# A plan of 26 rounds in place of 27 for the experts of a mixture, with a first batch of two rounds

## The chip, the cores and the metric

The kernel runs on one core of a Trainium2 chip. The metric is the device time of one execution in microseconds (us), the median of several runs. A profile was taken of one execution; its trace gives every instruction of the engines: PE (TensorE, matrix products), DVE (VectorE), ACT (ScalarE), POOL (GpSimd), and SP (SyncE), which here only issues DMAs.

## The reference

One layer of a backbone on 384 tokens (128 of context, 256 latent) of width 1024: a state space branch, a Fourier branch, and a mixture of 64 experts, of which a router gives six to each token. Only the mixture matters here:

```
scores = sigmoid(x @ w_router); idx = the six best of the four best groups
gates  = scores of idx, normed, * 2.5, else 0                 # (T, 64)
a = einsum("td,edf->tef", x, w1); b = einsum("td,edf->tef", x, w3)
act = silu(a) * b * gates[:, :, None]
routed = einsum("tef,efd->td", act, w2)                       # w1, w3: 1024x256, w2: 256x1024
x += gate2 * (routed + shared(x));  y = rms_norm(x)
```

All is float32. One expert's w1, w3 and w2 are 1 MiB each.

## The kernel before

Everything up to the router takes the first 490 us or so and is not touched. The last block of the kernel runs over the experts.

**Rounds and places.** Experts are sorted by how many tokens they got. A round is a tile of 128 rows (slots), which one to three experts share in blocks of 32 rows: `KINDS` has A with three experts of 2, 1, 1 blocks, B with two of 3 and 1, C with one of 4, D with two of 2 and 2. `PLAN` is a list of batches, each a string of rounds. Numbering the experts of the plan in order gives the places 0 to 63; `laid_out` gives the place with the most blocks to the expert with the most tokens. An expert with more tokens than its blocks hold would have the rest done by a dynamic loop (`Tail4`) behind the batches; on these inputs that loop runs no time. The plan of before has 27 rounds: three in the first batch, four in each of the six others.

**A batch** on PE: the gather (`L1700`: 48 matmuls, a column for each slot of the batch, takes the tokens of the slots out of H), then for each round p `hidden(p)` (`L1663`, w1 and w3 side by side, 1024 by 512), `turned(p)` (`L1670`, transposes), `slot_rows(p)` (`L1651`), `down(p)` (`L1684`, w2), and the scatter of two rounds at a time (`L1640`: six products of 512 columns to banks 0 and 1), whose results DVE adds to the sum (`add`, `L1828`). In a batch of four rounds the scatter of rounds 0 and 1 stands between `hidden(3)` and `down(2)`; that of rounds 2 and 3 comes in the next batch behind its `hidden(0)`. In the first batch of three, the scatter of rounds 0 and 1 stands behind `hidden(2)`.

The gather of a batch waits for the slots that DVE makes in `next_slots()`, and until the adds of the scatters issued before it are done (`pe.wait_ge(acc_ok, bt(12, -5))`).

**The weights.** Five slots of 3 MiB (`RING = 5`, the last is `sb_W`) hold the experts; place n lies in slot n % 5. The first four are loaded before the block. SP issues all other loads in program order, and stops at each whose slot is not free:

```
if place >= RING:
    sp.wait_ge(h_mm, round_of[place - RING] + 1)      # gate_up: w1 and w3
...
if place >= RING:
    sp.wait_ge(y1_mm, round_of[place - RING] + 1)     # downward: w2
```

For a batch of four rounds the order is gate_up 0, gate_up 1, downward 0, gate_up 2, downward 1, gate_up 3, downward 2, downward 3. Behind the last load SP waits for the last user of `sb_W` and issues there the stored activations (`x2_dram`, 1.5 MiB), the final gain (0.5 MiB) and, after that user's `down`, the gate `g2b` (1 MiB).

**The end.** In the last batch DVE does `add`, `before_residual(0)` (which waits for those three loads), the subtractions of `down(2)`, `before_residual(1)`, those of `down(3)`, `before_residual(2)`. PE's last scatter waits for the subtractions (`y_low`). Then come the last residual, the norm and the stores.

Of the kernel before, what the change touches and what calls it, by code (L numbers as in the profile page):

```python
# [49 lines left out]
N_CONST = 560  # L50

KINDS = dict(A=(2, 1, 1), B=(3, 1), C=(4,), D=(2, 2))
PLAN = ("CAB", "ADAB", "ABAD", "ABAB", "ADAB", "ADAB", "ABDC")
SB = 32


def laid_out():

    rounds, caps = [], []
    for batch in PLAN:  # L60
        rounds.append([])
# [15 lines left out]
ROUNDS, RANK = laid_out()  # L77
# [55 lines left out]
def build(nc, i, o):  # L133

    with ExitStack() as ctx:
# [1350 lines left out]
             "gates_ok", "tail_ok", "tail_step", "x3_ok", "y_ready")]  # L1486
        NB = len(PLAN)
        rounds_before = [sum(len(r) for r in ROUNDS[:b]) for b in range(NB)]
        assert all(len(r) == 4 for r in ROUNDS[1:]) and len(ROUNDS[0]) in (3, 4)
        y_bank = [(5, 6), (5, 6), (5, 6), (2, 1)]  # L1490

        def wait_last(eng, s, value):
# [65 lines left out]
        with nc.Block() as block:  # L1558
            @block.sync
            def _(sp):  # L1560
                round_of = [rounds_before[b] + p for b in range(NB) for p, r in enumerate(ROUNDS[b]) for _ in r]

                def gate_up(b, p):
                    for _, _, place in ROUNDS[b][p]:
                        if place >= RING - 1:
                            e = sp.value_load(ids64[:, place:place + 1], min_val=0, max_val=E - 1)  # L1566
                            if place >= RING:
                                sp.wait_ge(h_mm, round_of[place - RING] + 1)
                            load13(sp, place % RING, bass.ds(e, 1))

                def downward(b, p):
                    for _, _, place in ROUNDS[b][p]:
                        if place >= RING - 1:
                            e = sp.value_load(ids64[:, place:place + 1], min_val=0, max_val=E - 1)
                            if place >= RING:
                                sp.wait_ge(y1_mm, round_of[place - RING] + 1)
                            load2(sp, place % RING, bass.ds(e, 1))

                for b in range(NB):
                    gate_up(b, 0)  # L1580
                    gate_up(b, 1)
                    downward(b, 0)
                    if len(ROUNDS[b]) == 4:
                        gate_up(b, 2)
                        downward(b, 1)
                        gate_up(b, 3)
                        downward(b, 2)
                        downward(b, 3)
                    else:
                        downward(b, 1)  # L1590
                        gate_up(b, 2)
                        downward(b, 2)

                def half(pairs, expert):

                    for q in range(2):
                        sp.wait_ge(h_mm, pairs + (q - 1))
                        for k in (2 * q, 2 * q + 1):
                            load13(sp, k, expert(k))
                    for q in range(2):  # L1600
                        sp.wait_ge(y1_mm, pairs + (q - 1))
                        for k in (2 * q, 2 * q + 1):
                            load2(sp, k, expert(k))

                last = round_of[max(range(RING - 1, E, RING))] + 1
                sp.wait_ge(h_mm, last)
                sp.dma_start(X, x2_dram).then_inc(fin_in, 16)
                sp.dma_start(fin_g, i["final_norm_g"].partition_broadcast(P)).then_inc(fin_in, 16)
                sp.wait_ge(y1_mm, last)
                for r in range(2):  # L1610
                    sp.dma_start(g2b[:, r, :], ada_dram[r, 5 * D:6 * D].partition_broadcast(P)).then_inc(fin_in, 16)
                sp.wait_ge(tail_ok, 1)
                more = sp.value_load(ids[0:1, 0:1], min_val=0, max_val=MAXT // BATCH)
                with sp.If(more > 0):
                    sp.wait_ge(tail_ok, 2)
                    with sp.Fori(0, more) as b:
                        for x in range(2):
                            e = [sp.value_load(ids[0:1, bass.ds(b * BATCH + (TAIL_RING * x + k + 1), 1)], min_val=0, max_val=E - 1)
                                 for k in range(TAIL_RING)]
                            half(b * 4 + (N_ROUNDS + 2 * x), lambda k: bass.ds(e[k], 1))  # L1620
                sp.wait_ge(y_ready, 1)
                sp.dma_start(o["y_prompt"][0], OUT[:, 0]).then_inc(dram_out, 16)
                for j in (1, 2):
                    sp.wait_ge(y_ready, j + 1)
                    sp.dma_start(o["y_sample"][0, (j - 1) * P:j * P, :], OUT[:, j]).then_inc(dram_out, 16)
                sp.wait_ge(dram_out, 96)

            @block.tensor
            def _(pe):
                def scatter(B, base, rounds_done, ps):  # L1630

                    pe.wait_ge(slot_rows_ok, B.per_round(1, rounds_done))
                    pe.wait_ge(y_low, B.per_round(2, 2 * rounds_done))
                    for m in range(2 * NT):
                        j, h = divmod(m, 2)
                        if m == 0 or m >= 2:
                            pe.wait_ge(acc_ok, B.per_batch(12, base + max(m, 1)))
                        for p in ps:
                            for x in range(2):
                                ins = nc.tensor.matmul(bank[m % 2][:, :], ST[:, p, j * P:(j + 1) * P],  # L1640
                                                       YR[:, x, p % 2, 512 * h:512 * h + 512], start=p == ps[0] and x == 0,
                                                       stop=p == ps[-1] and x == 1)
                        ins.then_inc(scatter_mm, 1)

                def body(B):
# [57 lines left out]
                    pe.wait_ge(gates_ok, bt(1, 1))  # L1703
                    hidden(0)
                    if not B.first:
                        scatter(B, -6, 0, (2, 3) if B.tail or B.b > 1 else range(2, len(ROUNDS[0])))
                    slot_rows(0)
                    hidden(1)
                    turned(0)
                    slot_rows(1)  # L1710
                    down(0)
                    slot_rows(2)
                    if len(B.rounds) == 4:
                        hidden(2)
                        turned(1)
                        slot_rows(3)
                        down(1)
                        turned(2)
                        hidden(3)
                        scatter(B, 0, 2, (0, 1))  # L1720
                        down(2)
                        turned(3)
                        down(3)
                    else:
                        turned(1)
                        down(1)
                        hidden(2)
                        scatter(B, 0, 2, (0, 1))
                        turned(2)
                        down(2)  # L1730
                scatter(batches(pe, body), -6, 0, (2, 3))

            @block.scalar
            def _(act):
                def body(B):
# [27 lines left out]
                    turned(0)  # L1763
                    slot_rows(1)
                    down(0)
                    slot_rows(2)
                    if len(B.rounds) == 4:
                        hidden(2)
                        turned(1)
                        slot_rows(3)  # L1770
                        down(1)
                        turned(2)
                        hidden(3)
                        down(2)
                        turned(3)
                        down(3)
                    else:
                        turned(1)
                        down(1)
                        hidden(2)  # L1780
                        turned(2)
                        down(2)

                for j in range(NT):
                    nc.scalar.activation(Hh[:, j], H[:, j], ACT.Copy).then_inc(h_high_ok, 1)  # L1785
# [9 lines left out]
            def _(dve):  # L1795
# [101 lines left out]
                def body(B):  # L1897
# [45 lines left out]
                    gates(1)  # L1943
                    hidden(1)
                    down(0)
                    gates(2)
                    if n_rounds == 4:
                        hidden(2)
                        gates(3)
                        down(1)  # L1950
                        next_slots()
                        hidden(3)
                        add(bt, 0)
                        if B.last:
                            before_residual(0)
                        down(2)
                        if B.last:
                            before_residual(1)
                        down(3)
                        if B.last:  # L1960
                            before_residual(2)
                    else:
                        down(1)
                        next_slots()
                        hidden(2)
                        add(bt, 0)
                        down(2)

                TS = 3 + 5 * NT

# [91 lines left out]
```

## Time and profile before

| | us |
|---|---|
| median of 3 runs (lowest, highest) | 1018.99 (1016.47, 1020.28) |
| the profiled execution, its own time | 1019.57 |
| span of the profile, first to last instruction | 1017.8 |
| PE busy | 917.1 (90%) |
| DVE, ACT, POOL busy | 409.5, 199.1, 99.7 |
| read from HBM | 268.3 MB |

The page cuts the span into 40 equal slices; the loop over the experts begins in slice 20. In a timeline each line is a run of like instructions: its start, its length, engine, line, operation and count, and in brackets how long the engine stood idle before it and what ended that.

### The profile page before, as it was taken

How to read it: one execution, taken by the hardware profiler on the slowest of the kernel's cores; microseconds unless marked ns; L12 is line 12 of the kernel's file. 1: busy time of each engine (PE TensorE's matmuls, PEld its weight loads, DVE VectorE, ACT ScalarE, POOL GpSimd, SP SyncE). 2: the span in 40 equal slices, each digit the busy share in tenths (PEclk: the TensorE clock that was granted, in tenths of full speed). 3: DMA queues.
4: the chain of work that ended last, by engine and by line, in shares of the span. 5: the costliest groups of instructions: out<-in, count | busy, mean ns of one | idle time of the engine just before them, and what ended most of it. 6: DMA issues, size and time to landing. Idle time of an engine off the chain costs nothing.

```text
span 1017.8 us, 14342 instructions
## 1 busy us (share of the span) xinstructions
PE 917.1 (90%) x5681; PEld 500.2 (49%) x5681; DVE 409.5 (40%) x1009; ACT 199.1 (20%) x428; POOL 99.7 (10%) x100
## 2 busy tenths in 40 slices
PE   3639999999998999979799989989989989989994
PEld 2415757755675554436445435435435435435442
DVE  4399283599022133245413323223223223322247
ACT  4112514300122100141311111111112111111112
POOL 0699940000000000000000000000000000000000
PEclk9859899999997999979899999999999999999997
DMA  9945343420226513010799899999999999999951
GB/s 237 415 191 193 141 166 106 131 97 0 95 105 249 226 52 124 1 62 1 321 395 421 329 427 426 421 427 426 405 425 426 411 426 426 421 427 427 426 243 64
DMA packets 50088, 272.53 MB, mean 268 GB/s; under 512 B 5729, under 2 KB 14343, under 8 KB 21535
## 3 DMA queue, kind: packets, MB, share of 16 engines
q1 hardware_dynamic: 48706, 267.31, 64.4%
q10 hardware_dynamic: 1312, 4.25, 1.5%
q8 instruction: 47, 0.77, 0.3%
q14 instruction: 23, 0.19, 0.0%
HBM read 268.30 MB, written 3.24 MB: 267 GB/s over the span
## 4 chain that ended last, share of the span: by engine, by line
PE 37%; DMA 8%; issue 2%; SPq 2%; DVE 1%; ACT 1%; DVEq 0%
PE bank L1663 16%; PE bank L1684 8%; PE bank L1700 8%; DMA sb<-w 8%; PE bank L1640 5%; SPq L1067 1%; PE bank L1670 1%; ACT sb L1750 1%; ACT sb_Y L1755 0%; SPq L1566 0%; DVE sb_H L2014 0%; DVE sb L2022 0%; DVE sb L2034 0%; DVE sb_S L1816 0%; DVE sb_W L1895 0%
## 5 line engine op out<-in xcount | busy, mean ns | idle before, releaser
L1663 PE MATMUL bank<-sb 128*32 128x512 f32 (+2 forms) x1024 | 197.5, 612 | 7.2 <-DMA sb<-w 7.2
L1684 PE MATMUL bank<-sb 128*32 128x512 f32 (+2 forms) x512 | 98.3, 596 | 2.6 <-ACT sb L1750 2.6
L1663 PE MATMUL bank<-sb_W,sb 128*32 128x512 f32 (+1 forms) x448 | 88.2, 610 | 9.2 <-issue 9.2
L1663 PEld LDWEIGHTS bank<-sb 128*32 128x32 f32 (+2 forms) x1024 | 57.4, 117 | 71.6 <-issue 71.5
L1640 PE MATMUL bank<-sb_Y,sb_ST 128*128 128x512 f32 x324 | 86.5, 419 | 3.4 <-DVE sb_Y L1930 2.2
L1700 PE MATMUL bank<-sb_S,sb_H 128*128 128x512 f32 (+1 forms) x336 | 78.9, 394 | 5.7 <-ACT sb_H L1785 4.0
L701 PE MATMUL bank<-early 128*128 128x384 f32 x256 | 82.8, 486 | 0.0
L1828 DVE TENSOR_TENSOR sb<-sb,bank 128x512 f32<-128x512 f32 x78 | 53.7, 688 | 63.4 <-PE bank L1640 62.7
L1640 PEld LDWEIGHTS bank<-sb_Y,sb_ST 128*128 128x128 f32 x324 | 57.8, 193 | 37.2 <-issue 13.5
L1700 PEld LDWEIGHTS bank<-sb_S,sb_H 128*128 128x128 f32 x336 | 63.3, 194 | 24.3 <-issue 5.0
L1930 DVE TENSOR_TENSOR sb_Y<-bank,sb_Y 128x512 fp32r<-128x512 f32 x54 | 37.4, 692 | 72.8 <-ACT sb_Y L1755 72.7
L701 PEld LDWEIGHTS bank<-early 128*128 128x128 f32 x256 | 48.6, 190 | 33.9 <-issue 0.2
L1663 PEld LDWEIGHTS bank<-sb_W,sb 128*32 128x32 f32 (+1 forms) x448 | 26.4, 116 | 60.7 <-issue 60.2
L1755 ACT ACTIVATE sb_Y<-bank 128x512 fp32r<-128x512 f32 x54 | 32.3, 597 | 112.7 <-PE bank L1684 112.7
L1923 DVE SCALAR_TENSOR_TENSOR sb<-sb,bank 128x256 f32<-128x256 f32 x27 | 13.0, 480 | 95.5 <-ACT sb L1746 94.0
L1746 ACT ACTIVATE sb<-bank 128x256 f32<-128x256 f32 x27 | 10.4, 385 | 208.4 <-PE bank L1663 208.4
L609 PE MATMUL bank<-early 128*128 128x384 f32 x96 | 34.7, 517 | 15.5 <-ACT early L428 15.5
L1684 PE MATMUL bank<-sb_W,sb 128*32 128x512 f32 (+1 forms) x224 | 43.7, 596 | 4.3 <-ACT sb L1750 4.3
L1165 PE MATMUL bank<-sb 128*128 128x512 f32 x96 | 41.5, 593 | 1.7 <-DVE sb L1315 1.7
L1684 PEld LDWEIGHTS bank<-sb 128*32 128x32 f32 (+2 forms) x512 | 25.8, 114 | 32.2 <-issue 28.1
L1910 DVE COPY sb<-bank 128x512 f32<-128x512 f32 (+1 forms) x28 | 18.8, 673 | 55.1 <-PE bank L1700 55.1
L358 POOL TENSOR_TENSOR sb<-sb 128x192 f32<-128x192 f32 (+2 forms) x32 | 36.5, 1139 | 2.5
(289 smaller groups left out, 1120.1 us busy)
## 6 DMA issues: line engine op xcount, KB each, us to landing
sb<-w SPq DMA_DIRECT2D x156, 1024.0 KB, 17.3
sb_W<-w SPq DMA_DIRECT2D x36, 1024.0 KB, 15.8
sb<-w_ada SPq DMA_DIRECT2D x15, 1024.0 KB, 8.7
early<-w_in SPq DMA_DIRECT2D x12, 1024.0 KB, 10.3
early<-w_ada SPq DMA_DIRECT2D x9, 1024.0 KB, 24.6
sb<-w_out SPq DMA_DIRECT2D x1, 4096.0 KB, 17.1
sb<-ada_dram SPq DMA_DIRECT2D x6, 512.0 KB, 15.4
early<-w_proj_s SPq DMA_DIRECT2D x1, 2560.0 KB, 16.0
```

The lines of the kernel that those rows point to most:

```text
L358: pool.tensor_tensor(dest, dest, t, op).then_inc(cp_step, 1)
L609: ins = nc.tensor.matmul(mid_bank("u", f)[:, 0:TOK], w_a[c][:, f * P:(f + 1) * P], hT[:, c, :], start=c == 0, stop=c == KC - 1)
L701: ins = nc.tensor.matmul(bank[gate_bank[m % 2]][:, 0:TOK], w[:, c, P * (m % 2):P * (m % 2) + P], hT[:, c, :], start=c == 0, stop=c == KC - 1)
L1165: ins = nc.tensor.matmul(bank[4 + n][:, :], GLT[:, m, j * P:(j + 1) * P], w_o[:, m, 512 * n:512 * n + 512], start=m == 0, stop=m == KC - 1)
L1640: ins = nc.tensor.matmul(bank[m % 2][:, :], ST[:, p, j * P:(j + 1) * P], YR[:, x, p % 2, 512 * h:512 * h + 512], start=p == ps[0] and x == ...
L1663: ins = nc.tensor.matmul(bank[2 + p % 2][c0:c0 + w, :], XT[:, c, P * p + c0:P * p + c0 + w], slot13[k][:, :, c, :], start=c == 0, stop=c = ...
L1684: ins = nc.tensor.matmul(bank[y_bank[p][h]][c0:c0 + w, :], hidT[:, f, c0:c0 + w], slot2[k][:, f, 512 * h:512 * h + 512], start=f == 0, sto ...
L1700: ins = nc.tensor.matmul(bank[c % 2][:, 0:B.slots], part[:, j, c * P:(c + 1) * P], S[:, j, 0:B.slots], start=j == 0 and x == 0, stop=j == ...
L1755: nc.scalar.activation(YR[:, 0, p % 2, 512 * h:512 * h + 512], bank[y_bank[p][h]][:, :], ACT.Copy).then_inc(y_high, 1)
L1828: tt(ACC[:, j, 512 * h:512 * h + 512], ACC[:, j, 512 * h:512 * h + 512], bank[m % 2][:, :], ALU.add).then_inc(acc_ok, 1)
L1910: nc.vector.tensor_copy(XT[:, c, 0:B.slots], bank[1][:, 0:B.slots]).then_inc(xt_dve, 1)
L1930: tt(YR[:, 1, p % 2, cols_], bank[y_bank[p][h]][:, :], Y[:, 0, p % 2, cols_], ALU.subtract).then_inc(y_low, 1)
```

## The change

The plan has 26 rounds, 14 of them of kind A (three experts), in place of 27 with 12 of kind A. The first batch has two rounds, so 256 slots in place of 384. All six other batches end in a round of kind A, behind a round of two experts in five of them, and the last batch ends in two rounds of kind A; before, four of the five middle batches ended in B and one in D, and the last in D and C. The third round of the first batch goes from each engine's program; the scatter of round 0 alone stands behind `down(1)` there, and that of round 1 in the next batch. On DVE `next_slots()` comes ahead of the subtractions of `down(1)` in the first batch. The plan has two places of 4 blocks (two before), 7 of three blocks (8 before), 20 of two (22) and 35 of one (32).

```diff
--- before.py
+++ after.py
@@ -50,7 +50,7 @@
 N_CONST = 560
 
 KINDS = dict(A=(2, 1, 1), B=(3, 1), C=(4,), D=(2, 2))
-PLAN = ("CAB", "ADAB", "ABAD", "ABAB", "ADAB", "ADAB", "ABDC")
+PLAN = ("CA", "BADA", "BABA", "DABA", "CABA", "BADA", "ABAA")
 SB = 32
 
 
@@ -1486,7 +1486,7 @@
              "gates_ok", "tail_ok", "tail_step", "x3_ok", "y_ready")]
         NB = len(PLAN)
         rounds_before = [sum(len(r) for r in ROUNDS[:b]) for b in range(NB)]
-        assert all(len(r) == 4 for r in ROUNDS[1:]) and len(ROUNDS[0]) in (3, 4)
+        assert all(len(r) == 4 for r in ROUNDS[1:]) and len(ROUNDS[0]) == 2
         y_bank = [(5, 6), (5, 6), (5, 6), (2, 1)]
 
         def wait_last(eng, s, value):
@@ -1588,8 +1588,6 @@
                         downward(b, 3)
                     else:
                         downward(b, 1)
-                        gate_up(b, 2)
-                        downward(b, 2)
 
                 def half(pairs, expert):
 
@@ -1703,14 +1701,14 @@
                     pe.wait_ge(gates_ok, bt(1, 1))
                     hidden(0)
                     if not B.first:
-                        scatter(B, -6, 0, (2, 3) if B.tail or B.b > 1 else range(2, len(ROUNDS[0])))
+                        scatter(B, -6, 0, (2, 3) if B.tail or B.b > 1 else (1,))
                     slot_rows(0)
                     hidden(1)
                     turned(0)
                     slot_rows(1)
                     down(0)
-                    slot_rows(2)
                     if len(B.rounds) == 4:
+                        slot_rows(2)
                         hidden(2)
                         turned(1)
                         slot_rows(3)
@@ -1724,10 +1722,7 @@
                     else:
                         turned(1)
                         down(1)
-                        hidden(2)
-                        scatter(B, 0, 2, (0, 1))
-                        turned(2)
-                        down(2)
+                        scatter(B, 0, 1, (0,))
                 scatter(batches(pe, body), -6, 0, (2, 3))
 
             @block.scalar
@@ -1763,8 +1758,8 @@
                     turned(0)
                     slot_rows(1)
                     down(0)
-                    slot_rows(2)
                     if len(B.rounds) == 4:
+                        slot_rows(2)
                         hidden(2)
                         turned(1)
                         slot_rows(3)
@@ -1777,9 +1772,6 @@
                     else:
                         turned(1)
                         down(1)
-                        hidden(2)
-                        turned(2)
-                        down(2)
 
                 for j in range(NT):
                     nc.scalar.activation(Hh[:, j], H[:, j], ACT.Copy).then_inc(h_high_ok, 1)
@@ -1943,8 +1935,8 @@
                     gates(1)
                     hidden(1)
                     down(0)
-                    gates(2)
                     if n_rounds == 4:
+                        gates(2)
                         hidden(2)
                         gates(3)
                         down(1)
@@ -1960,11 +1952,9 @@
                         if B.last:
                             before_residual(2)
                     else:
+                        next_slots()
                         down(1)
-                        next_slots()
-                        hidden(2)
                         add(bt, 0)
-                        down(2)
 
                 TS = 3 + 5 * NT
```

## Rows read from the trace of the kernel before

**Rows 1.** The page, busy tenths in 40 slices of the span.

```profile
PE   3639999999998999979799989989989989989994
...
DMA  9945343420226513010799899999999999999951
```

**Rows 2.** Windows by batch: us, busy of each engine, PE's granted clock, DMA share, GB/s.

```profile
852.00:926.00 74.00, 69.57 (x457) 33.12 (x454) 22.04 (x43) 11.90 (x25) 0.00 (x0) 1.00 1.01 425
926.00:995.00 69.00, 68.11 (x380) 33.19 (x378) 24.27 (x40) 11.54 (x24) 0.00 (x0) 1.00 0.82 342
```

**Rows 3.** The page, DMA issues of the experts' weights.

```profile
sb<-w SPq DMA_DIRECT2D x156, 1024.0 KB, 17.3
sb_W<-w SPq DMA_DIRECT2D x36, 1024.0 KB, 15.8
```

**Rows 4.** Timeline of PE, end of the sixth batch, start of the last.

```profile
911.48 6.07 PE L1640 MATMUL bank<-sb_Y,sb_ST 128*128 128x512 f32 x24
...
936.94 7.07 PE L1663 MATMUL bank<-sb 128*32 128x512 f32 x64
943.94 6.11 PE L1640 MATMUL bank<-sb_Y,sb_ST 128*128 128x512 f32 x24
...
958.26 3.64 PE L1684 MATMUL bank<-sb 128*32 128x512 f32 x32 [0.17 <-ACT sb L1750]
```

**Rows 5.** Timeline of PE, first three batches.

```profile
527.93 3.70 PE L1684 MATMUL bank<-sb 128*128 128x512 f32 x8 [0.17 <-ACT sb L1750]
...
553.90 11.34 PE L1700 MATMUL bank<-sb_S,sb_H 128*128 128x512 f32 x48
...
572.17 1.20 PE L1640 MATMUL bank<-sb_Y,sb_ST 128*128 128x512 f32 x4
573.69 3.10 PE L1640 MATMUL bank<-sb_Y,sb_ST 128*128 128x512 f32 x8 [0.32 <-DVE sb L1828]
...
591.04 8.77 PE L1663 MATMUL bank<-sb 128*32 128x512 f32 x64 [1.88 <-DMA sb<-w]
...
665.74 7.08 PE L1663 MATMUL bank<-sb 128*32 128x512 f32 x64 [1.86 <-DMA sb<-w]
```

**Rows 6.** Timeline of SP, first loads, a blocked one, the end.

```profile
487.97 0.84 SPq L1067 DMA_DIRECT2D sb<-w  x2
...
572.45 4.01 SPq L1067 DMA_DIRECT2D sb<-w  x6
...
965.12 0.43 SPq L1607 DMA_DIRECT2D sb_W<-x_dram  x1
...
974.02 0.80 SPq L1611 DMA_DIRECT2D sb_W<-ada_dram  x2
```

**Rows 7.** Windows around the blocked load and the end of the queue.

```profile
572.00:574.00 2.00, 1.68 (x9) 1.00 0.26 33
574.00:576.00 2.00, 1.88 (x6) 1.00 0.92 369
980.00:982.00 2.00, 2.00 (x7) 1.00 0.66 270
```

**Rows 8.** Windows of PE with its granted clock.

```profile
504.00:508.00 4.00, 4.00 (x17) 0.67 1.01 426
508.00:512.00 4.00, 4.00 (x25) 1.00 1.01 426
580.00:600.00 20.00, 17.95 (x127) 0.91 1.01 426
```

**Rows 9.** Timeline of the end, DVE's residual and PE's last scatter.

```profile
987.72 1.22 DVE L1894 TENSOR_TENSOR sb<-sb,sb_W 128x1024 f32<-128x1024 f32 x1
...
990.24 0.69 DVE L1930 TENSOR_TENSOR sb_Y<-bank,sb_Y 128x512 fp32r<-128x512 f32 x1
...
997.53 3.21 PE L1640 MATMUL bank<-sb_Y,sb_ST 128*128 128x512 f32 x8 [2.19 <-DVE sb_Y L1930]
```

## The prediction

> **What bounds the kernel now.** I read the page's slices first: from slice 21 on, which is the loop over the experts, PE and the DMA engines both stand mostly at 9 tenths [rows 1]. Both can't be the bound by busy time alone, so I read the loop batch by batch: in a full batch of the middle the DMA engines are at 1.00 to 1.01 with 425 GB/s, in the last at 0.82 [rows 2]. The sizes say why: 156 + 36 issues of 1024 KB [rows 3] are 192 MiB for 64 experts, 3 MiB each (2 for w1 and w3, 1 for w2). At 426.5 MB/ms (425 to 427 in the full stretches) one MiB takes 2.46 us. Four rounds with ten experts are 30 MiB, 73.8 us.
>
> PE's own work for four rounds is less. From PE's timeline [rows 4, 5]: gather 11.3, four hidden products of 7.0, two scatters of 6.0 to 6.1, four down products of 3.6, and some 4 us of transposes, slot rows and waits for ACT: 70.0 us. So in the middle the queue of weights sets the pace (73.8), PE waits for it one or two times a batch, and only after the last weights does PE's rest set the end. PE time that is taken out of the middle is therefore worth nothing by itself. What counts is when the queue stands empty. It does so where SP, which issues in program order, stops at a load whose slot isn't free: SP issues the loads of places 11 to 13 at 572.45 [rows 6], 0.2 us after the first hidden product of batch 1 (the scatter behind it starts at 572.17 [rows 5]), and the queue is nearly empty in the 2 us behind that (33 GB/s) and full again after it [rows 7]. The 31 MiB before place 11 take 76.2 us from the first byte at 489.8 (SP issues from 487.97 [rows 6]); with some 2 us lost at place 5 they end at 568. So before loses about 6 us there.
>
> **A tool for the sum: the latency of a load that SP was blocked on.** 0.2 us to the issue; 572.45 to the first byte at about 574.1 by the bytes of the windows 572 to 576 [rows 7]; 6 MiB, 14.8 us, end at 588.9; PE starts on them at 591.04 [rows 5]. That is 0.2 + 1.7 + 2.1 = 4.0. Taking 3.0 instead makes the walk below, applied to the kernel before, end 3 us early; 3.6 (0.2 + 1.9 + 1.5) ends it at 1019.0 for the measured 1017.8, with its seven gathers within 1.5 us of the trace. I take 3.6, bounds 3.0 and 4.0.
> A second term: behind its wait at 591.04 the hidden product takes 8.77 us instead of 7.07, and the clock granted in that stretch is 0.91, where 1.2 GHz stood for part of it instead of 2.4 [rows 5, 8]. That is 1.7 us. The wait of 1.86 us at 665.74 is followed by 7.08 [rows 5]. Of seven waits of 1.8 to 2.5 us that I read off the same timeline, from 591.04 to the last at 904.48, five had it. I charge 1.7 for every wait above 1.8 us. The Trainium skill (TensorE: Matmul & The Clock Gate, section on HAM oscillation) has it that each long enough wait for a DMA makes the next group of matmuls start at half rate, at a cost of half the throttled time. It speaks against a change that lengthens such waits; five of seven rows agree, and the rows alone would spare one or two of them, 2 to 3 us of the sum.
>
> **The first batch: two rounds, 256 columns.** A hidden product, a down product and a third of the gather go. At full clock 25 matmuls of 384 columns took 4.00 us, 0.16 each; from 504 to 508, partly at the low clock, 17 [rows 8]. With 256 columns 0.107 each when the clock is up. The gather then ends at 510.5 (bounds 509.8, and 512.9 as now). Hidden 0 to 517.0, hidden 1 held by the bytes of place 3 until 518.2 and done at 525.2, transposes and slot rows 1.0, down 0 3.2 (one expert, eight matmuls as in [rows 5]), 1.3, down 1 to 534.3. Here the change adds a wait. The scatter of round 0 stands directly between down 1 and the next gather, and that gather waits for all six adds of DVE. DVE has the slots of batch 1 and the two subtractions of down 1 ahead of them. Before, a scatter of one round took PE from 572.17 to 576.79 with a stop for an add [rows 5], 4.6 us; for the queue on DVE I add 3.0 (bounds 1.0 and 4.0: two subtractions of 0.69, two copies of ACT and the last add). The gather of batch 1 starts at 542.0, against 553.90 [rows 5]: PE gains 12 us.
>
> **But the queue loses them at once.** With two rounds in batch 0, place 9's load waits for place 4's round, which is now the first of batch 1, behind its gather. What SP can issue before it is 12 MiB for experts 0 to 3, 10 for w1 and w3 of 4 to 8, and 2 for w2 of 4 and 5: 24 MiB, 59.0 us, dry at 548.8. Place 4's round is through at 542.0 + 11.3 + 7.0 = 560.3, first byte at 562.4. Idle 13.6 us, where before lost 6 + 2. The remaining 168 MiB take 413.1 us: 975.5 if nothing else stops.
>
> **The batch boundaries.** From the end of a fourth hidden product to the end of the next batch's first one pass 32.5 us (911.5 to 944.0 [rows 4]): scatter, two down products, gather, hidden. Now each batch but the first ends in a round of three experts. PE waits for its last weights, so from their last byte to the restart of the queue pass 1.5 + 7.0 + 1.7 + 32.5 + 2.1 = 44.8 us. In that time SP can issue, before it stops at a place that needs the next batch's first round: w2 of the third and fourth round (5 MiB), w1/w3 of the next first and second round (10), w2 of the first (2): 17 MiB, 41.8 us, idle 3.0. With the order of before (third A, fourth B, next A, then D or B) the same count gives 18 MiB, 44.3 us, idle 0.6. Boundary by boundary: 3.0, 3.0, into CABA 16 MiB and a hidden of 6.5, so 5.0, and 1.2 inside that batch (place 40 waits for place 35), then 3.0, and 0.6 into ABAA. Sum 15.8, where before has 0.6 five times. Byte end 991.3 so far.
>
> **The end: two rounds of three on a ring of five.** Place 63 uses the slot of place 58, which is now in round 2 of the last batch. (1) Its w1/w3 can be issued only when hidden 2 is through; hidden 3 waits for them. The last 6 MiB are w2 of 58 to 62 and of 63, so w1/w3 of 63 are there at 991.3 - 14.8 + 1.5 = 978.0 and hidden 3 ends 8.7 later, scatter 6.0, down 2 3.6: 996.4. (2) Only then may w2 of 63 be issued: first byte 998.5, the queue has been dry for 9.7 us, byte end 1001.0, down 3 is done at some 1006. (3) Behind it in SP's order stand the stored activations, the final gain and the gate: 1.5 + 0.5 + 1.0 MiB. Before they went at 965.12 and 974.02 [rows 6] and the queue was through at 982 [rows 7]; DVE began on them at 987.72 without a wait [rows 9]. Now they end at 1001.0 + 7.4 = 1008.4, seen at 1009.4. DVE stands before them in its first residual, with the subtractions of rounds 2 and 3 queued behind it, and PE's last scatter needs those: 2.5 (residual 0) + 1.4 + 2.5 + 1.4 + 0.8 = 8.6 [rows 9]. The last scatter starts at 1018.0; before at 997.53 [rows 9]. What follows is untouched, 20.2 us.
>
> **Sum.** 1018.0 + 20.2 = 1038.2 span; less the 1.2 by which the same walk is long for before: 1037. The profiled execution of before had 1019.57 for a span of 1017.80 and lies 0.6 above the median of the runs shown (1018.99): 1037 + 1.8 - 0.6 = 1038. A measurement of this kernel tells a difference from about 0.5%, 5 us.
>
> **The rivals.**
> - The same, with smaller losses, 1029: latency 3.0 and no low clock behind the waits takes 9 us off the sum; so does an end in which the residual's loads are not what DVE waits for (last scatter 2.2 us behind down 3, 1008, span 1028.5). Against the first: 4.0 at place 11, 8.77 at 591.04. The Trainium skill (DMA: Bandwidth & Descriptors, Anatomy of one DMA) gives a fixed part of about 2.0 us for a DMA; by it alone this case would be the result, and the 4.0 read here is against it. Chance 0.18.
> - More, 1043: waits of 5 to 7 us before fourth hidden products are longer than any in this loop now, and if the low clock costs 2.6 instead of 1.7 behind each, it comes to 4 to 5 us more. Chance 0.12.
> - Faster, 999: the queue doesn't run dry. Then the bytes end at 489.8 + 472.1 = 961.9, residual loads 969.3, +1.0 + 8.6 + 20.2 = 999. PE could do it (542.0 + 6 x 70.0 = 962). For it the order of SP would have to be no obstacle; 39.1 us of idle would have to shrink below 19 to break even. For it speaks that 27 rounds to 26 takes some 14 us off PE. Against it is SP's stop at 572.45. Chance 0.05.
> - No change, within 5 us, where half of the idle is avoided: 0.03.
> - An expert that no longer fits its capacity, so that the loop for overflow runs: a batch of four rounds, 74 us as the gathers are apart, and its first loads from a dry queue, some 17: 1110. Routing the reference's inputs gives 109, 108, 90, 88, ... tokens, 63 for the tenth expert and 30 for the thirtieth. The new plan gives them 64 and 32. Chance 0.02.
>
> My forecast has 0.60. Slower 0.92, same 0.03, faster 0.05. The range 1024 to 1047 takes in both smaller and larger losses.
>
> **What would show it.** Gather of batch 1 near 542 and a stop of the queue of 13 to 14 us around 555; gathers then 76 to 77 us apart, 72 for the batch with C; a wait of about 5 us before most fourth hidden products; a wait before hidden 3 of the last batch of about 7 us; SP's issue for place 63's w2 after 990; DVE idle until about 1009. I am wrong if gathers follow each other in 74 us or less, or if DVE's first residual starts right behind the last add.

## The result and the profile after

The changed kernel takes 1044.38 us (median of 4 runs, 1041.96 to 1044.88), the kernel before beside it 1018.29 us. The ratio is 1.024, 95% interval 1.0223 to 1.0258: 26 us slower, where 1038 was forecast and 1024 to 1047 was the range. The profiled execution took 1044.28 us with a span of 1042.5.

The page of the changed kernel, busy tenths in 40 slices, answers to [rows 1]:

```profile
PE   3739999999999999889789799799799999799753
...
DMA  9935245220509303002995998998997999999941
GB/s 247 415 162 218 108 162 173 71 81 0 194 2 380 133 1 121 38 23 101 427 425 225 427 427 359 427 427 352 427 426 313 418 427 401 427 426 419 421 167 61
```

PE's and the DMA engines' rows both have lower digits through the loop. The last row dips to 225, 359, 352, 313 and 401 between slices of 427, about once a batch: there the queue runs dry. The same over one full batch, of which [rows 2] has the like before (1.01 and 425 GB/s):

```profile
618.00:696.00 78.00, 71.35 (x500) 32.29 (x500) 21.72 (x44) 11.72 (x24) 0.00 (x0) 0.96 0.96 404
```

PE's timeline, the lines that answer to [rows 5] and, for the last batch, to [rows 9]:

```profile
540.45 11.16 PE L1698 MATMUL bank<-sb_S,sb_H 128*128 128x512 f32 x48 [0.94 <-DVE sb L1820]
...
594.65 9.51 PE L1661 MATMUL bank<-sb 128*32 128x512 f32 x64 [7.14 <-DMA sb<-w]
...
979.83 9.77 PE L1661 MATMUL bank<-sb 128*32 128x512 f32 x64 [7.58 <-DMA sb<-w]
...
1004.36 6.02 PE L1682 MATMUL bank<-sb 128*32 128x512 f32 x32 [4.75 <-DMA sb<-w]
1021.54 3.77 PE L1638 MATMUL bank<-sb_Y,sb_ST 128*128 128x512 f32 x8 [11.16 <-DVE sb_Y L1922]
1026.17 5.69 PE L1638 MATMUL bank<-sb_Y,sb_ST 128*128 128x512 f32 x16 [0.86 <-DVE sb L2012]
```

The second gather starts at 540.45, 13 us ahead of before's 553.90. The first fourth hidden product starts 7.14 us late for its weights and then takes 9.51 us; four more waits of 5.4 to 7.6 us follow, one a batch, but for the batch with C, where it is 1.9. The seven gathers start at 499.7, 540.5, 618.3, 696.6, 775.0, 846.4 and 923.1: 77 to 78 us apart in full batches, 71 for CABA, where the forecast had 76 to 77 and 72. In the last batch hidden 3 waits 7.58 us, down 3 waits 4.75 us, and the last scatter stands 11.16 us for DVE.

SP's timeline (start, time, issues), which answers to [rows 6]:

```profile
558.82 0.81 SPq L1067 DMA_DIRECT2D sb_W<-w  x2
...
971.21 28.50 SPq L1070 DMA_DIRECT2D sb<-w  x4
999.75 0.43 SPq L1605 DMA_DIRECT2D sb_W<-x_dram  x1
...
1000.70 1.23 SPq L1609 DMA_DIRECT2D sb_W<-ada_dram  x2
```

558.82 is place 9, issued 0.2 us after place 4's hidden product. The line at 971.21 is a run of four w2 issues that lasts 28.50 us: its last one, place 63, had to wait until down 2 was through at 999.2 and was issued at 999.4. Behind it, at 999.75, come the residual's loads, 34.6 us later than in before (965.12).

Windows of that time, the last column GB/s; they answer to [rows 7]:

```profile
548.00:550.00 2.00, 2.00 (x10) 1.00 0.14 57
550.00:552.00 2.00, 2.00 (x13) 1.00 0.00 0
...
556.00:558.00 2.00, 2.00 (x24) 1.00 0.00 0
558.00:560.00 2.00, 1.74 (x12) 1.00 0.19 33
560.00:562.00 2.00, 1.82 (x6) 1.00 0.78 299
...
634.00:638.00 4.00, 4.00 (x34) 1.00 0.21 68
988.00:1000.00 12.00, 11.61 (x74) 1.00 0.20 83
1000.00:1002.00 2.00, 0.00 (x0) 1.00 0.71 213
1008.00:1010.00 2.00, 2.00 (x16) 0.70 1.00 324
1010.00:1012.00 2.00, 0.38 (x4) 1.00 0.80 322
```

Counting the bytes that are missing at 427 GB/s, the queue is empty from about 548.3 to 560.5: 12 us. Around 636 it is empty for about 4 us. From 988 to 1000 it moves 83 GB/s, 1.0 MB, which is 2.3 us of work, and from 1000 to 1002 one us of work: empty from 990.3 to 1001.0. The last two windows are the end of the loads behind the weights, at 324 and 322 GB/s; windows of one us in the last section show what lies in them.

DVE at the end:

```profile
995.64 0.69 DVE L1820 TENSOR_TENSOR sb<-sb,bank 128x512 f32<-128x512 f32 x1 [0.24 <-PE bank L1638]
1013.88 1.23 DVE L1886 TENSOR_TENSOR sb<-sb,sb_W 128x1024 f32<-128x1024 f32 x1 [17.56 <-DMA sb_W<-ada_dram]
...
1016.40 1.29 DVE L1922 TENSOR_TENSOR sb_Y<-bank,sb_Y 128x512 fp32r<-128x512 f32 x2
...
1020.12 1.29 DVE L1922 TENSOR_TENSOR sb_Y<-bank,sb_Y 128x512 fp32r<-128x512 f32 x2
```

The residual waits 17.56 us for the gate's load, the subtractions that PE's last scatter needs come behind it in DVE's order, and the last scatter starts at 1021.54, 24.0 us after before's 997.53. The rest of the span is 21.0 us, 20.3 before.

### The profile page after: what moved, and what is told of

It reads as the page before. It is cut to its first block, busy times and chain, and to the rows that moved or that the text cites. A ratio compares the mean times of both kernels' runs of the same rounds, so it can differ in the third digit from the quotient of the medians.

```text
span 1042.5 us, 14297 instructions
## 1 busy us (share of the span) xinstructions
PE 909.3 (87%) x5664; PEld 490.1 (47%) x5664; DVE 407.6 (39%) x1006; ACT 196.4 (19%) x423; POOL 99.9 (10%) x100
## 4 chain that ended last, share of the span: by engine, by line
PE 46%; DMA 15%; DVE 3%; SPq 3%; ACT 2%; issue 2%; DVEq 0%
PE bank L1661 14%; DMA sb<-w 13%; PE bank L1698 6%; PE bank L1638 6%; PE bank L1682 5%; PE bank L1165 4%; PE bank L1154 3%; PE bank L1142 2%; PE bank L1187 2%; SPq L1067 2%; DMA sb_W<-ada_dram 1%; PE bank L1156 1%; ACT early L1268 1%; PE bank L1180 1%; DVE sb L1820 1%
## 5 line engine op out<-in xcount | busy, mean ns | idle before, releaser
L1661 PE MATMUL bank<-sb 128*32 128x512 f32 (+2 forms) x1152 | 188.7, 639 | 34.1 <-DMA sb<-w 34.1
L1661 PEld LDWEIGHTS bank<-sb 128*32 128x32 f32 (+2 forms) x1152 | 53.7, 119 | 123.1 <-issue 122.5
L1682 PE MATMUL bank<-sb 128*32 128x512 f32 (+2 forms) x576 | 93.4, 613 | 10.3 <-ACT sb L1745 5.5
L1638 PE MATMUL bank<-sb_Y,sb_ST 128*128 128x512 f32 x312 | 85.0, 423 | 13.6 <-DVE sb_Y L1922 11.2
L1661 PE MATMUL bank<-sb_W,sb 128*32 128x512 f32 (+2 forms) x320 | 84.8, 594 | 0.0
L1698 PE MATMUL bank<-sb_S,sb_H 128*128 128x512 f32 (+1 forms) x336 | 76.4, 388 | 6.9 <-ACT sb_H L1777 4.0
L1682 PEld LDWEIGHTS bank<-sb 128*32 128x32 f32 (+2 forms) x576 | 24.3, 114 | 49.4 <-issue 41.4
L1682 PE MATMUL bank<-sb_W,sb 128*32 128x512 f32 (+2 forms) x160 | 43.7, 596 | 0.7 <-ACT sb L1745 0.7
L1661 PEld LDWEIGHTS bank<-sb_W,sb 128*32 128x32 f32 (+2 forms) x320 | 23.6, 118 | 29.5 <-issue 29.2
```

Of the source, the lines that this page charges most:

```text
L1661: ins = nc.tensor.matmul(bank[2 + p % 2][c0:c0 + w, :], XT[:, c, P * p + c0:P * p + c0 + w], slot13[k][:, :, c, :], start=c == 0, stop=c = ...
L1682: ins = nc.tensor.matmul(bank[y_bank[p][h]][c0:c0 + w, :], hidT[:, f, c0:c0 + w], slot2[k][:, f, 512 * h:512 * h + 512], start=f == 0, sto ...
L1698: ins = nc.tensor.matmul(bank[c % 2][:, 0:B.slots], part[:, j, c * P:(c + 1) * P], S[:, j, 0:B.slots], start=j == 0 and x == 0, stop=j == ...
```

## The experiments

Names with a_ start from the changed kernel, those with b_ from the kernel before. Each was timed beside the kernel before, whose median was 1018.65 (a_order to a_w1only), 1018.46 (b_w1only to b_best) and 1018.22 us (a_best, b_best_dve). The walk spoken of in the expectations is the prediction's way to add up, done for every load and every product: the loads in SP's order at 2.46 us a MiB, PE's program with the durations of the rows. Two of its terms were set anew by the profile after: 2.5 us for the low clock behind a wait above 4 us, and 1.5 in place of 3.0 us for DVE's queue before the second gather. That it then ends at the changed kernel's own span, 1042.5, is therefore no test of it; the runs below are.

**a_order: SP's order in a batch.**

```diff
                         gate_up(b, 0); gate_up(b, 1); downward(b, 0)
...
-                        gate_up(b, 2)
                         downward(b, 1)
+                        gate_up(b, 2)
                         gate_up(b, 3)
```

> The changed kernel with one edit in SP's program: in batches of four rounds downward 1 is issued ahead of gate_up 2. If the loss is the queue running dry while SP stands at the w1/w3 of a place that needs the next batch's first round (theory), 3 MiB, 7.4 us, more are in the queue across each gather: the stop of about 14 us before the gather of batch 1 is over shrinks to about 6, those of 4 us at the later boundaries go, waits before the fourth hidden products fall from 5 to 6 us to 1 to 3. The walk gives 1028.5 us, 16 less than the changed kernel; the end stays as it is, with the last scatter some 22 us behind down 2 of the last batch. If the loss is in PE's own order (the scatter before the gather in the first batch, rounds of three experts that cost PE more), the time stays within 3 us of 1044.

Measured 1026.68 us, 18 less than the changed kernel; ratio to before 1.0062 (1.0041 to 1.0082). Its windows of the first stop:

```profile
556.00:558.00 2.00, 2.00 (x24) 1.00 0.96 406
558.00:560.00 2.00, 2.00 (x24) 1.00 0.13 53
560.00:562.00 2.00, 2.00 (x16) 1.00 0.00 0
562.00:564.00 2.00, 1.63 (x6) 1.00 0.69 193
```

The queue is empty from about 558.3 to 563.0, 4.8 us in place of 12, and the gathers start at 502.2, 543.1, 613.0, 688.4, 760.5, 831.9 and 907.2. PE's work is the same to the last instruction, so an edit of SP's order alone takes back 18 of the 26 us, by keeping the queue full for longer across the gathers. The end is unchanged: last gather to last scatter 97.4 us, 98.5 in the changed kernel.

**a_spread: rounds of three not last in the batches.**

```diff
-PLAN = ("CA", "BADA", "BABA", "DABA", "CABA", "BADA", "ABAA")
+PLAN = ("CA", "ADAB", "ABAB", "ADAB", "ABAC", "ADAB", "ABAA")
```

> The changed kernel with its 26 rounds in another order: CA, ADAB, ABAB, ADAB, ABAC, ADAB, ABAA. Same kinds, same first batch of two, same last batch; only the middle batches end in a round of two experts or one. Theory: 18 MiB in place of 17 stand before SP's stop at a boundary, and a wait before the fourth hidden product of 2 to 3 us in place of 5 to 6, so the gathers are 74.3 us apart in place of 78; the walk gives 1028 us. Rival (the loss is the first batch and the end alone): 1044 within 3 us.

Measured 1027.9 us; ratio to before 1.0087 (1.0055 to 1.012). Gathers at 498.4, 539.1, 613.6, 688.3, 761.3, 831.4, 904.8: the first full batches are 74.4 and 74.7 us apart, with waits of 2.4 and 2.5 us before the fourth hidden products. By the missing bytes the queue stands empty for 9.6 us at the first stop (12 in the changed kernel) and for 0.8 and 0.4 us at the next two boundaries (4.0 and 4.6), and for 2.8 around the batch with C. The placing of the rounds alone, same kinds and same last batch, is worth some 16 us.

**a_dve: the residual behind the subtractions on DVE.**

```diff
-                        if B.last:
-                            before_residual(0)
                         down(2)
-                        if B.last:
-                            before_residual(1)
                         down(3)
                         if B.last:
-                            before_residual(2)
+                            for j in range(NT):
+                                before_residual(j)
```

> The changed kernel with DVE's three before_residual of the last batch behind the subtractions of down 3. Theory: the last scatter no longer waits for the loads of the residual and starts some 2.2 us behind down 3, at 1012.6 in place of 1021.5; but its sums are added by DVE only behind the residuals, which start with the loads at 1013.9 and take 7.4 us, so the first final product starts at about 1021.5 in place of 1025.4: 4 us less, 1040.5. If DVE's wait for the loads is not what sets the end, nothing changes (1044).

Measured 1042.57 us, 1.8 less, within the spread of the runs of both (1040.52 to 1044.22 here); the profiled one has a span of 1039.5, 3.0 less. PE's last scatter in it:

```profile
1012.77 3.78 PE L1638 MATMUL bank<-sb_Y,sb_ST 128*128 128x512 f32 x8 [3.86 <-issue]
1023.10 6.20 PE L1638 MATMUL bank<-sb_Y,sb_ST 128*128 128x512 f32 x16 [6.54 <-DVE sb L2009]
```

It starts at 1012.77 as expected, then stops for 6.54 us for DVE, whose residuals start with the loads at 1013.20 and let the first final product go at 1022.35 (1025.43 in the changed kernel). The wait was there, and without it the scatter starts 8.8 us earlier. But the residuals can't start before the loads are in (here 0.7 us earlier than in the changed kernel, which the edit doesn't explain), and the final products stand behind them. The times alone are inconclusive; the trace shows that the late loads set the end.

**a_w1only and b_w1only: a third of the bytes away.** In both kernels w3 is not loaded and w1 is used in its place; PE does as many matmuls.

```diff
         for n, w in enumerate((w1, w3)):
-            sp.dma_start(slot[k][:, 2048 * n:2048 * n + 2048], w[:, e, :]).then_inc(w13_in[k], 16)
+            sp.dma_start(slot[k][:, 1024 * n:1024 * n + 1024], w1[:, e, 1024 * n:1024 * n + 1024]).then_inc(w13_in[k], 16)
...
-                                                       slot13[k][:, :, c, :], start=c == 0, stop=c == KC - 1)
+                                                       slot13[k][:, 0:1, c, :].to_broadcast([P, 2, FE]), start=c == 0, stop=c == KC - 1)
```

> The changed kernel with w1 used in place of w3, which is not loaded: 2 MiB an expert in place of 3 and the same number of matmuls on PE. Theory (bytes and their order set the pace): now PE does; the gather of the last batch comes at about 888, no wait before hidden products but in the last batch, gathers 70 us apart; the end stays slow (w2 of place 63 and the residual's loads behind down 2), so about 1000 us. Rival, PE's own order: no gain over the pace of 76 to 78 us a batch.

> The kernel before with w1 used in place of w3, which is not loaded, as in the run of that kind on the changed kernel. Theory: PE sets the pace, the gather of the last batch comes at about 903.5, 15 to 16 us behind the changed kernel's with the same edit: that is what the 27th round is worth where PE is the bound. The end has no late load (last scatter 2.2 us behind down 3), so about 998.5 us: no slower than the changed kernel of this kind, which gives its lead back at its end. Rival (the 26 rounds cost PE more than they save): its last gather is not behind.

Measured 997.56 us on the changed kernel (ratio to before 0.9789, 0.9754 to 0.9823) and 994.61 us on the kernel before (0.9763, 0.9737 to 0.9789). Gathers of full batches are 70 us apart in both. One batch of each, a_w1only first, with the DMA engines at 0.78 and PE busy for 69.09 of 70 us:

```profile
608.00:678.00 70.00, 69.09 (x505) 31.82 (x502) 22.02 (x43) 11.75 (x25) 0.00 (x0) 1.00 0.78 300
621.00:691.00 70.00, 69.09 (x456) 32.00 (x452) 22.04 (x43) 11.72 (x24) 0.00 (x0) 1.00 0.78 299
```

The last gather starts at 886.9 in the first and 900.8 in the second: with PE as the bound, the plan of 26 rounds is 13.9 us ahead there. Then it gives the lead back and ends 3 us later. The last scatter of the changed kernel's version, then that of before's:

```profile
975.21 3.40 PE L1638 MATMUL bank<-sb_Y,sb_ST 128*128 128x512 f32 x8 [12.12 <-DVE sb_Y L1922]
```

```profile
972.90 3.12 PE L1640 MATMUL bank<-sb_Y,sb_ST 128*128 128x512 f32 x8 [2.48 <-issue]
```

Down 3 is through at 963.1 and the scatter waits 12.12 us for DVE, which waits for the residual's loads; in the other it is 2.48.

**b_end: the last batch of the change in the kernel before.**

```diff
-PLAN = ("CAB", "ADAB", "ABAD", "ABAB", "ADAB", "ADAB", "ABDC")
+PLAN = ("CAB", "ADAB", "ABAD", "ABCB", "ADDB", "ADAB", "ABAA")
```

> The kernel before, 27 rounds with its first batch of three, in the order CAB, ADAB, ABAD, ABCB, ADDB, ADAB, ABAA: only the last batch is that of the change (two rounds of three experts at the end), C and D move to batches 3 and 4. Theory: about the pace of before in the middle (one stop of some 10 us at place 39, behind batch ABCB with its eight experts), a wait of some 7 us before hidden 3 of the last batch, w2 of place 63 issued behind down 2, DVE's residual waiting for its loads: 1035.5 us by the walk, 17 more than before. Rival (the end costs nothing, only the first batch does): within 5 us of 1018 plus the stop at place 39, below 1025.

Measured 1034.71 us; ratio 1.0156 (1.0119 to 1.0192). Its end in PE's timeline:

```profile
971.65 9.59 PE L1663 MATMUL bank<-sb 128*32 128x512 f32 x64 [7.93 <-DMA sb<-w]
...
995.90 5.98 PE L1684 MATMUL bank<-sb 128*32 128x512 f32 x32 [4.65 <-DMA sb<-w]
1013.04 3.77 PE L1640 MATMUL bank<-sb_Y,sb_ST 128*128 128x512 f32 x8 [11.16 <-DVE sb_Y L1930]
```

The three waits of the changed kernel's end are all there, 7.93, 4.65 and 11.16 us. Last gather (913.9) to last scatter (1013.0) takes 99 us; in the kernel before 71.8 (925.68 to 997.53). The earlier gather has its reason in the same edit, since three experts more are loaded in the last batch and so three less before it. The stop expected at place 39 came too: by the missing bytes the queue is empty for 10 us from 780 to 791, and for 3 us more around 859. Net the edit costs 16 us, and as the stop at place 39 comes from moving C and D, these are not the price of the last batch alone.

**b_order: the order of SP in the kernel before.** The edit of a_order.

> The kernel before with downward 1 issued ahead of gate_up 2. Theory: the stop of 6 us at place 11 shrinks to about 1, and the waits of about 2.5 us before the fourth hidden products move to the third or go; the walk gives 1014 span, 1015.5 us, 3 to 5 less than before. Rival (order of SP is no part of it): 1018 within 2.

Measured 1015.93 us, median of 10; ratio 0.9973 (0.9955 to 0.9991). Batch 1 takes 70.2 us from gather to gather, where it took 73.1; the four behind it take 74.3 to 75.3 as before. The stop at place 11 shrinks from 5.8 us to 1.1, and no more than that is gained: the waits before the fourth hidden products are gone, but those before the third are 2.6 to 3.7 us.

**b_best: 27 rounds, SP's order and another plan.**

```diff
-PLAN = ("CAB", "ADAB", "ABAD", "ABAB", "ADAB", "ADAB", "ABDC")
+PLAN = ("ACA", "ACDA", "ADBA", "BACA", "ADBA", "ADCA", "ABBA")
...
-                        gate_up(b, 2)
                         downward(b, 1)
+                        gate_up(b, 2)
```

> The kernel before with 27 rounds, a first batch of three, downward 1 ahead of gate_up 2, and the plan ACA, ACDA, ADBA, BACA, ADBA, ADCA, ABBA, found with the same walk: rounds of three experts at the start of the last batch and a round of two before its last, no place whose slot is freed by the round just before it. Theory: the queue hardly runs dry, bytes end near 962, PE's end sets the time, 999 span, 1001 us. Rival (the walk leaves out something that matters as soon as the queue is full): above 1010.

Measured 1004.87 us; ratio 0.9863 (0.9835 to 0.9891). The windows of its seven batches, columns as in [rows 2]:

```profile
500.00:553.00 53.00, 49.92 (x303) 26.04 (x301) 16.64 (x33) 8.29 (x18) 0.00 (x0) 0.95 1.01 426
553.00:621.00 68.00, 66.58 (x372) 31.28 (x368) 24.03 (x54) 11.57 (x24) 0.00 (x0) 1.00 1.01 427
621.00:692.00 71.00, 69.89 (x457) 32.67 (x454) 22.07 (x44) 11.89 (x25) 0.00 (x0) 1.00 1.01 426
692.00:762.00 70.00, 68.47 (x430) 33.79 (x429) 21.86 (x42) 11.68 (x25) 0.00 (x0) 1.00 1.01 426
762.00:833.00 71.00, 68.76 (x453) 32.18 (x452) 22.02 (x43) 11.44 (x25) 0.00 (x0) 1.00 1.01 426
833.00:903.00 70.00, 68.42 (x381) 34.05 (x382) 21.85 (x42) 11.62 (x25) 0.00 (x0) 1.00 1.01 426
903.00:970.00 67.00, 65.29 (x468) 30.94 (x467) 17.95 (x35) 10.61 (x22) 0.00 (x0) 1.00 0.97 410
```

The DMA engines are at 1.01 to the last batch: the queue no longer runs dry, and the batches take 70 us. They have nine or ten experts each, 27 to 30 MiB, so that the queue needs 66 to 74 us for one: PE and the queue are now nearly even. This plan has 14 rounds of three experts, as many as the change, beside 5 of B, 4 of C and 4 of D. PE's end:

```profile
970.50 3.64 PE L1684 MATMUL bank<-sb 128*32 128x512 f32 x32 [0.56 <-ACT sb L1750]
982.72 3.77 PE L1640 MATMUL bank<-sb_Y,sb_ST 128*128 128x512 f32 x8 [8.57 <-DVE sb_Y L1930]
```

The last scatter still stands 8.57 us for DVE, which sees the gate's load at 975.07. Plan and order were changed together here; of the 13.6 us gained, b_order shows 2.5 for the order by itself.

**a_best and b_best_dve.** The first is the changed kernel with SP's new order and the plan below, the second is b_best with the DVE edit of a_dve.

```diff
-PLAN = ("CA", "BADA", "BABA", "DABA", "CABA", "BADA", "ABAA")
+PLAN = ("AC", "ADAA", "ABDA", "ABCA", "ABBA", "BADA", "BABA")
```

> The changed kernel's 26 rounds and first batch of two with what the earlier runs showed to be better: downward 1 ahead of gate_up 2, and the order AC, ADAA, ABDA, ABCA, ABBA, BADA, BABA, the best the walk finds for 26 rounds: no two rounds of three experts at the end. Theory: the end is as short as before (residual loads not late by more than 1 to 2 us), the stop before the second gather's end shrinks to 4 us, some waits stay because 14 rounds of three experts in 26 can't all be kept apart by others on a ring of five; 1015.5 us, so 26 rounds are no better than 27 even then. Rival (only the order was at fault, 26 rounds are worth their 14 us): 1003 or less.

> The kernel of b_best with DVE's three before_residual of the last batch behind the subtractions of down 3. In b_best DVE waits for the gate's load until 975.1, the last scatter starts at 982.7, 8.6 us behind down 3. Theory: it starts at about 976.3 instead, the residuals end at 982.6, the first final product starts there in place of 986.6: 4 us less, 1001 us. Rival (the last residual and norm hide it): 1005 within 1.

a_best took 1024.65 us, median of 6 (1019.64 to 1025.78); ratio 1.0059 (1.0039 to 1.0079). It is 9 us above the walk. The profiled run is the fastest of the six, at a span of 1017.8; what the others lose was not seen. Its end isn't as short as expected: the residual's loads were to be late by no more than 1 to 2 us, but DVE stands 8.53 us for the gate's load, until 989.77, and PE's last scatter 8.71 us for DVE. One of its other waits is of another kind, and the walk has it at the same place (5.0 us):

```profile
614.46 1.08 PE L1682 MATMUL bank<-sb 128*32 128x512 f32 x3 [4.73 <-DMA sb_W<-w]
```

a down product that waits for its w2, held up behind w1 and w3 of later places. The queue stands empty for some 7 us around 607 there. Of the orders tried, none with 26 rounds is faster than the kernel before. b_best_dve took 1003.45 us (ratio 0.9847, 0.9817 to 0.9877), 1.4 less than b_best, where 4 were expected; the runs of both overlap (1002.37 to 1004.54 and 1003.48 to 1005.96), so the time alone doesn't show a gain. In the trace the last scatter starts at 978.22, 4.5 us earlier, but the first final product starts only 1.1 us earlier, at 985.55, because the residuals don't start with the load at 975 but behind the subtractions of down 3, at 976.40, and take 7.5 us. It is the fastest version run, 1.5% below the kernel before.

| kernel | expected us | measured us |
|---|---|---|
| a_order | 1028.5 | 1026.7 |
| a_spread | 1028 | 1027.9 |
| a_dve | 1040.5 | 1042.6 |
| a_w1only | 1000 | 997.6 |
| b_w1only | 998.5 | 994.6 |
| b_end | 1035.5 | 1034.7 |
| b_order | 1015.5 | 1015.9 |
| b_best | 1001 | 1004.9 |
| a_best | 1015.5 | 1024.7 |
| b_best_dve | 1001 | 1003.5 |

## Why the prediction was right, and by how much it was off

**The bound.** The queue of weights sets the middle, as forecast: a_order and a_spread, with the same rounds on PE, take 16 to 18 us off, and with a third fewer bytes the batches fall to PE's 70 us.

**The first batch.** Forecast were 542.0 for the second gather and 13.6 us of an empty queue; measured 540.45 and 12. The term of 3.0 us for DVE's queue was too large: the scatter and its adds took 6.1 us in place of 7.6.

**The boundaries.** The forecast had stops of 3.0, 3.0, 5.0 and 1.2, 3.0 and 0.6 us, 15.8 in all. From the bytes missing in windows around them I read about 4.0, 4.6, 6.5, 0.9, 1.5 and 0.5, 18.0 in all; the places are right. The first three are longer, in part (0.7 to 1.0 us each) because of the next term; the fifth is half of what was forecast.

**The low clock.** This is the term of the sum that was mis-sized. I charged 1.7 us for each wait. The count behind it was off by one: PE's timeline of before has six waits of 1.82 to 2.54 us, not seven, and four of them, not five, had the extra 1.7. Behind waits of 5.4 to 7.6 us the hidden product took 9.51, 9.71, 9.81, 8.51 and 9.77 us, so 1.4 to 2.7 us more than 7.07, on average 2.4. Clock windows of the changed kernel (the granted clock stands behind the bracket, 0.50 is 1.2 GHz throughout), and behind them two of the kernel before, at its wait of 1.88 us:

```profile
594.00:598.00 4.00, 3.35 (x16) 0.50 1.01 428
598.00:602.00 4.00, 4.00 (x36) 0.80 1.01 426
602.00:606.00 4.00, 4.00 (x31) 1.00 1.02 428
...
591.00:592.00 1.00, 0.96 (x12) 1.00 1.07 451
592.00:593.00 1.00, 1.00 (x12) 0.51 1.00 426
```

PE was idle for 7.14 us until 594.65. At all five waits the clock was down to 0.50 by the time PE restarted, and it stayed there for 2.9 to 5.5 us more, by windows of one us; half of that is what the products took longer. In the kernel before PE restarted at 591.04 with the clock still at 1.00, and it stood at 0.50 only from 592 to about 595.5. The Trainium skill's rule (TensorE: Matmul & The Clock Gate, HAM oscillation) that each long wait for a DMA ends in a cold start was right in all five; what I took for the price came from the shorter waits of before.

The forecast's span was 1037, the measured one is 1042.5. Stretch by stretch the 5.5 us are, each rounded:

| | us more than the sum had |
|---|---|
| to the second gather | -1.6 |
| four hidden products behind long waits, to the last batch | 2.5 |
| the rest up to hidden 3 of the last batch | 0.9 |
| hidden 3 of the last batch (1.1 behind its wait), scatter and down 2 | 1.0 |
| down 2 to the residual's loads | 1.7 |
| DVE's part before the last scatter | -0.9 |
| the rest of the span | 0.8 |
| the 1.2 taken off because the walk was long for before | 1.2 |

So the low clock is the largest term, 2.5 + 1.1 = 3.6 us, and the case that came is nearer to "more, 1043", to which I gave 0.12, than to the forecast.

**The end.** Steps (1) to (3) all came: hidden 3 at 979.83 (978.0 forecast), down 2 through at 999.2 (996.4), queue empty for 10.7 us (9.7), down 3 at 1004.36 and, at the low clock, 6.02 us long in place of 3.6, the residual's loads seen at 1013.88 (1009.4), last scatter at 1021.54 (1018.0). Of the 4.5 us at the loads 2.8 come with down 2; the 4 MiB from there on took 11.1 us and not 9.8, and DVE saw them 1.8 us behind their last byte, not 1.0; the first byte came 0.3 us sooner. DVE's part was 7.7 us and not 8.6.

**The rivals.** "Faster, 999" fell: there is an obstacle in SP's order. b_best shows that it can be taken away, and that the time near 1000 is then reached, but with 27 rounds. "Smaller losses, 1029", with the fixed 2.0 us of the Trainium skill (DMA: Bandwidth & Descriptors, Anatomy of one DMA), fell too. The page gives that figure for one DMA issued by GpSimd, and here SP issues them. For one load on an empty queue it is near all the same: w2 of place 63, issued at 999.4, was used at 1004.36, 2.5 us beside the 2.46 of its data. For the 6 MiB at place 11 the rows of before have 4.0, and it is such loads that stand in the middle of the kernel. The overflow loop did not run.

What stays open: why the median of a_best is 9 us above the walk and its runs differ by 6 us, and how much of the 16 us of b_end is the last batch and how much the moved C and D. A first batch of two was not tried with everything else held, since 27 rounds can't be cut so by this kernel.

## What to carry to other kernels

Where weights stream through a ring in one program order, count the bytes that can be issued before the next blocked load and hold them against the time until its slot comes free: 17 MiB or 18 before a gather was the difference between stops of 4.0 and 4.6 us and of 0.8 and 0.4. A load that is free to go must not stand in the order behind one that isn't, and what the very end waits for (here the residual's loads) should not be queued behind the last weights. Work saved on an engine that waits for the queue is worth nothing by itself: the round saved here is worth 14 us where PE is the bound (a_w1only against b_w1only), and the plan that saves it was 26 us slower, because SP could issue less ahead of its stops.

## What the runs showed of the hardware

- In the changed kernel, a_order and a_spread, PE's next hidden product took 1.4 to 2.7 us more behind waits of 4.3 to 7.6 us, and 0 or 1.7 us more behind waits of 1.6 to 3.1 us. Single waits of the other runs fall outside: 2.81 us cost 2.9 us in a_best, 7.99 us cost 1.7 in a_dve. So long waits cost more on average, and no single one can be priced by its length.
- The two cases differ in when the clock falls: behind a wait of 1.88 us it was still at 1.00 for the first us of the next product and then at 0.50 for some 3.5 us, behind one of 7.14 us it was at 0.50 from the first matmul to about 599.5.
- Behind the last w2 of the changed kernel come the stored activations (1.5 MiB), the final gain (0.5 MiB) and the gate (1 MiB), the last two one row of memory spread over all partitions. In windows of one us:

```profile
1006.00:1007.00 1.00, 1.00 (x12) 0.50 1.05 442
1008.00:1009.00 1.00, 1.00 (x8) 0.50 0.98 238
1009.00:1010.00 1.00, 1.00 (x12) 0.90 1.02 410
```

By the count of bytes the gate's load is what moves from 1009 on, at 410 and 418 GB/s, about the rate of the weights. What is slow, though the engines are busy, are the two us before it, 315 and 238 GB/s, where the activations end and the final gain moves. The same dip stands in a_dve, a_spread and b_end (lowest 262, 229 and 287 GB/s). What makes it was not tried.
